# One 128x256 copy on ScalarE moved three instructions earlier in the MLP loop of a four-layer transformer kernel

## The reference

```
h = rms_norm(x, mlp_norm_w)                      # 512 x 1024
x = x + square(relu(h @ w_up)) @ w_down          # w_up 1024 x 4096, w_down 4096 x 1024
```

## Time and profile before

| | us |
|---|---|
| median of 3 runs | 2474.54 |
| lowest and highest | 2473.72, 2476.83 |
| the profiled execution, its own time | 2473.49 |
| its span, first to last instruction | 2471.7 |

### The profile page before, as it was taken

The page is one execution under the profiler, slowest core; times in us unless marked ns, Lnnn a source line. Parts: engine busy times, 40 slices in busy tenths (PEclk is TensorE's granted clock), DMA queues, the critical chain, the costliest instruction groups (busy, mean ns, idle before and its releaser), DMA issues. The chain is left out here.

```text
span 2471.7 us, 32545 instructions
## 1 busy us (share of the span) xinstructions
PE 2367.4 (96%) x12840; PEld 1953.7 (79%) x12840; DVE 1291.4 (52%) x2210; ACT 1044.0 (42%) x1654; POOL 1204.7 (49%) x915
## 2 busy tenths in 40 slices
PE   8999999899999999998999999999999999999998
PEld 6776688788877767887888777888888868888887
DVE  4777685464437776845644544622223768422224
ACT  5345563342343456533334544522223566422223
POOL 4425286765534252766656355264435326434442
PEclk9999999999999999999999999999999999999999
DMA  5222122322322131323223122142223213223331
GB/s 168 69 69 94 52 86 86 102 86 86 99 73 86 60 103 35 102 71 112 74 86 119 64 69 84 37 136 85 95 94 120 86 51 103 86 86 103 102 102 52
DMA packets 153975, 214.58 MB, mean 87 GB/s; under 512 B 7776, under 2 KB 94944, under 8 KB 153568
## 3 DMA queue, kind: packets, MB, share of 16 engines
q1 hardware_dynamic: 153824, 212.51, 26.5%
HBM read 208.30 MB, written 2.10 MB: 85 GB/s over the span
## 5 line engine op out<-in xcount | busy, mean ns | idle before, releaser
L414 POOL TENSOR_TENSOR w_lo<-raw,w_hi 128x512 fp32r<-128x512 f32 (+1 forms) x648 | 834.1, 1323 | 1002.7 <-ACT w_hi L353 987.7
L452 PE MATMUL ps<-h_hi,w_hi 128*128 128x512 f32 (+1 forms) x1248 | 507.4, 407 | 10.2 <-POOL w_lo L414 10.1
L452 PE MATMUL ps<-h_hi,w_lo 128*128 128x512 f32 (+1 forms) x1248 | 487.6, 391 | 0.0
L452 PE MATMUL ps<-h_lo,w_hi 128*128 128x512 f32 (+1 forms) x1248 | 487.4, 391 | 0.0
L452 PE MATMUL ps<-hid_hi,w_hi 128*128 128x512 f32 x928 | 366.9, 395 | 10.2 <-POOL w_lo L414 4.7
L452 PE MATMUL ps<-hid_hi,w_lo 128*128 128x512 f32 x928 | 361.6, 390 | 0.0
L452 PE MATMUL ps<-hid_lo,w_hi 128*128 128x512 f32 x928 | 361.4, 389 | 0.0
L353 ACT ACTIVATE w_hi<-raw 128x2048 fp32r<-128x2048 f32 (+2 forms) x145 | 247.5, 1726 | 233.4 <-PE ps L452 99.1
L452 PEld LDWEIGHTS ps<-h_hi,w_hi 128*128 128x128 f32 (+1 forms) x1248 | 234.6, 188 | 71.7 <-issue 18.0
L452 PEld LDWEIGHTS ps<-h_lo,w_hi 128*128 128x128 f32 (+1 forms) x1248 | 234.4, 188 | 51.1 <-issue 5.6
L452 PEld LDWEIGHTS ps<-h_hi,w_lo 128*128 128x128 f32 (+1 forms) x1248 | 233.9, 187 | 51.4 <-issue 0.2
(11 more groups left out here) (355 smaller groups left out, 4454.4 us busy)
## 6 DMA issues: line engine op xcount, KB each, us to landing
raw<-in_w_down SPq DMA_DIRECT2D x32, 1024.0 KB, 5.0
raw_u<-in_w_up SPq DMA_DIRECT2D x28, 1024.0 KB, 5.2
raw<-in_ffn_w_gate SPq DMA_DIRECT2D x44, 512.0 KB, 3.8
raw<-in_ffn_w_up SPq DMA_DIRECT2D x44, 512.0 KB, 4.7
raw<-in_w_in SPq DMA_DIRECT2D x20, 1024.0 KB, 5.0
raw<-in_ffn_w_down SPq DMA_DIRECT2D x20, 1024.0 KB, 4.9
raw<-in_w_out SPq DMA_DIRECT2D x8, 1024.0 KB, 5.1
raw<-in_ev_w_in SPq DMA_DIRECT2D x8, 1024.0 KB, 5.1
```

The source lines that it names most:

```text
L414: pool.tensor_tensor(slot.lo(k)[:, 0:slot.width], raw[r][:, k, 0:slot.width], slot.hi(k)[:, 0:slot.width].bitcast(F32), ALU.subtract).then ...
L452: mm = pe.matmul(o, lh, rh, start=first and q == 0, stop=last and q == 2, skip_group_check=True)
```

## The change

In the ScalarE list of turns 2 to 7 the copy of the second half's first product moves ahead of the three rows of down slot 2 that stood before it. All four rows of that slot then stand together. No instruction is added or removed, and no other engine's list changes; the two landing buffers and the nine cells are as they were.

```diff
                         p1_copy(j, 0)
                         units_hi(act, ua + 1, 3, 7)
                     rows_hi(act, ua + 2, 0, 4)
-                    rows_hi(act, ua + 3, 0, 3)
                     if j >= 2:
                         p1_copy(j, 1)
-                    rows_hi(act, ua + 3, 3, 4)
+                    rows_hi(act, ua + 3, 0, 4)
                     for n in range(4):
                         squared(j, n)
```

## The result

The changed kernel takes 2394.65 us in the median of 4 runs (2394.34 to 2396.15), the kernel before 2474.88 beside it: a ratio of 0.968, 95% interval 0.966 to 0.969, some 80 us or 3.2% faster. The forecast was 2401 with a range of 2396 to 2413.

What follows compares the result with a forecast made beforehand. TensorE, busy 96%, bounds the kernel with its waits, chiefly 55.9 us before unit 4 in twelve turns. Gap 4.82 plus clock 1.30 is 6.12 us per turn, 73.4 in all, giving 2401 us, range 2396 to 2413.

Steps and rivals of the forecast that it cites:

- What released unit 4: TensorE's unit 4 of the second half waits for ScalarE's late copy of unit 0, not for GpSimd's line 414.
- The gap: TensorE's wait before unit 4 of the second half goes: 4.66 + 0.16 = 4.82 us per turn, twelve turns.
- the clock term: TensorE's slow multiplications after the wait at unit 4 return to full clock: gain 1.30 us per turn, twelve turns.
- The check from the period: One turn lasts 47.80 us, its work at full clock 41.9, so 5.9 us gained, against 6.12 summed.
- The lower end of the range: 2396 us, if the other eleven turns' gaps on TensorE also hid small idle times of weight loads.
- some 5 us more: Extra gain if small idle times of weight loads hide in the other eleven turns' gaps on TensorE, giving 2396.
- The covers: After T, the turn's first multiplication: work hidden behind TensorE, 1.7 us room at down slot 1, 6.5 at slot 2.
- the rival: Part of the wait returns at down slot 1, VectorE slowing GpSimd: 1.3 us per turn, about 2417; chance 0.05.
- no effect: GpSimd releases unit 4 as the list says, the copy is not the cause: nothing changes, 2474.5 us; chance 0.03.
- the plug: On ScalarE the moved copy holds up a landed down slot 2 if its product is late: 2480 us; chance 0.03.

Runs made afterwards that it cites:

- the copy by VectorE: Kernel before, with VectorE instead of ScalarE making the second copy, ScalarE's down-slot rows left where they were: 2394.54 us, ratio 0.967.
- the kernel with the fillers: Kernel before plus 36 extra unread multiplications on TensorE ahead of unit 4 of the second half in turns 2 to 7: 2452.91 us, ratio 0.991.
- two extra writes: Changed kernel, GpSimd writing the first low part of down slot 1 twice more in turns 2 to 7: 2396.92 us, ratio 0.969.
- five: Changed kernel, GpSimd writing the first low part of down slot 1 five times more in turns 2 to 7: 2456.01 us, ratio 0.993.

## Why the prediction was right in kind and wrong in size

- *What released unit 4* held. The list of waits named GpSimd; the copy it was. Three rows of other engines said so ahead of the change, and the copy by VectorE shows it.
- *The gap*, 4.82 us per turn, held to the hundredth. Start to start the twelve gaps of the trace of before sum to 59.3 us, less one slot of 0.12 each is 57.8, and the kernel with the fillers, which keeps the gaps, lies 58 us above the changed one.
- *The step that failed is the clock term*, "Gain 1.30 us per turn". It was read off one turn and multiplied by 12. That turn is the mildest of the twelve (5.59 us, with the one before it at 5.60). The stretches from the end of the gap to the down product, all the same 36 multiplications, in the kernel before:

```profile
393.62:399.84 6.22, 6.22 (x37) 6.22 (x37) 4.69 (x7) 2.79 (x5) 4.05 (x3) 0.66 0.53 173
442.44:448.19 5.75, 5.75 (x36) 5.75 (x37) 4.69 (x7) 2.79 (x5) 4.07 (x3) 0.73 0.46 155
490.56:496.16 5.60, 5.60 (x36) 5.60 (x37) 4.69 (x7) 2.79 (x5) 4.07 (x3) 0.75 0.50 171
...
586.20:593.30 7.10, 7.10 (x36) 7.10 (x37) 4.88 (x7) 2.94 (x6) 4.06 (x3) 0.57 0.59 195
...
1214.25:1221.35 7.10, 7.10 (x36) 7.10 (x37) 4.89 (x7) 2.94 (x6) 4.06 (x3) 0.57 0.60 193
...
sum 74.87, PE 74.85 PEld 74.87 DVE 56.82 ACT 33.80 POOL 48.80; mean PE 6.24 PEld 6.24 DVE 4.74 ACT 2.82 POOL 4.07
```

  The mean is 6.24 us against 4.27 at full clock (516.56 to 520.83 in the changed kernel): 1.97 per turn, 23.6 in all, 8 more than the forecast had. (About 0.1 of the 1.97 is not the clock: with the fillers these units take 4.38 us at a granted clock of 1.00.) With it the sum is 12 x (4.82 + 1.97) = 81.5, where the two traces differ by 81.4, and the time 2393. The check from the period missed it, because it used the period of the same turn; I noted that this turn was below the mean and put that down to its gap. The lower end of the range took "some 5 us more" for idle times that don't exist (from 373.13 to 641.97 TensorE idles 268.84 - 241.07 = 27.77 us in the kernel before, which is the sum of its six gaps); the real spread of the known term, from 1.3 to 2.8 per turn, was not in it.
- *The 1.6 us by which the median lies above 2393.* In the trace of the changed kernel the span is 77.3 us shorter and not 81.4. Of the 4.1, 2.1 are in turn 1 of the first layer, 47.69 us against 45.56, where the clock fell around the small waits that both kernels have there (in the down product of this turn 0.87 against 1.00); the rest lies behind both layers, 1155.32 against 1153.42. This profiled execution is the slowest of the four. Its causes are not told apart further.
- *The covers* held. The copy ran at T+11.7 (T+11.8 forecast), the down product started at T+20.05 (20.1), the turn took 41.84 (41.9), GpSimd began the next up slot at T+26.0 (26.5). Down slot 1 was done at T+18.9, for which the neighbourhood of VectorE cost 0.5 us as in the rival; two extra writes show that 2.7 us more cost only 0.2 us per turn, five that the rival is real beyond that.
- *The rivals* of no effect and of the plug did not come up: ScalarE waits 1.3 us for its product and then still 6.4 for the slot.

## What to carry to other kernels

An instruction of an in-order engine that others wait for should not stand behind one that waits for a DMA: one row of the landed slot ahead of it costs nearly as much as three, and so the move is worth the wait for the landing, not the rows' own time. When a wait names an engine whose result the waiter doesn't read, look for another engine that was released within a few tenths of a microsecond by the same signal. A gap on TensorE has a second price, the low clock behind it, and that price differs from turn to turn after equal gaps: sum it over all turns with a table by stretch, and let the range hold the spread.

## What the runs showed of the hardware

- After gaps of 4.77 to 5.32 us between starts, TensorE ran its next 36 multiplications in 5.59 to 7.10 us, with a granted clock of 0.75 to 0.57 in these stretches, a mix of 1.2 and 2.4 GHz. The length of the gap doesn't explain it: 4.86 us was followed by 7.10, 5.32 by 5.77. After gaps of 3.76 to 3.96 the clock fell in ten turns of twelve and not in two. The Trainium skill, in TensorE: Matmul & The Clock Gate (Part 1: The HAM clock gate, What's actually happening), says that the monitor runs on its own time and isn't restarted when a kernel starts, so that the point of the change shifts. The spread after nearly equal gaps agrees with that; no run here shows the monitor itself.
- Short waits can cost the clock too, and not each time. The down product of turn 1 in the changed kernel, first and second layer, behind the same two first waits of 0.9 and 0.7 us:

```profile
348.78:375.36 26.58, 25.68 (x97) 19.76 (x97) 20.26 (x22) 12.23 (x22) 22.57 (x15) 0.87 0.35 116
985.53:1009.98 24.45, 22.72 (x96) 17.87 (x97) 19.58 (x21) 12.25 (x22) 22.55 (x15) 1.00 0.31 96
```

- A filler keeps the clock: 36 multiplications per turn in the idle time made the kernel 22.5 us faster though the gaps stayed. Where a gap cannot be closed, that is worth having.
- Low parts of 128x512 on GpSimd took 1.24 us each with VectorE idle (4.96/4 in the earlier trace rows) and 1.37 to 1.49 with it active (5.47/4 and 5.96/4 in the changed kernel).
